# A hybrid decoder layer in float32 pairs: the pooling map goes into the output weight, kept weight parts load from the sync queue

## The chip, the cores and the metric

The kernel runs on one core of a Trainium2 chip. The metric is the device time of one execution in microseconds (us). Five engines work beside each other: TensorE (PE in the profile, its weight loads PEld), VectorE (DVE), ScalarE (ACT), GpSimd (POOL) and SyncE (SP), which here only issues DMAs. A DMA is issued by one of these engines and sits in that engine's queue. Engines meet through semaphores: each runs its own program in order, and what stands behind a wait in it waits too.

## The reference

One decoder layer over 2048 positions of 1024 features, in float32:

```python
z = rmsnorm(h, g_attn) @ w_in              # q (512), k (128), v (128), u (512)
a = sliding_window_sink_attention(norm(q), norm(k), v, sinks, rel_bias)   # window 128, 8 heads of 64
for g, w in enumerate((2, 4, 8, 16)):      # 4 groups of 128 channels
    pooled[g] = mean of the last w positions of u[g] - u[g]
m = einsum('bsgc,gcd->bsgd', pooled, w_pool) * pool_scale
h = h + concatenate([a, m]) @ w_out
h = h + (silu(hn @ w_gate) * (hn @ w_up)) @ w_down           # hn = rmsnorm(h, g_ffn), width 2816
h = h + sigmoid(rmsnorm(h, g_ple) @ w_ple_gate) * (p @ w_ple_proj)
```

## The kernel before

Every float32 operand of a matmul is kept as two parts, hi and lo (`_hi` is a rounded copy, made by ScalarE; `_lo` is the rest, made by VectorE: operand minus hi), and a product is three matmuls: hi x hi, hi x lo, lo x hi. The 2048 positions are four tiles of T = 512.

**Order.** TensorE goes through z(0), z(1), out(0), z(2), out(1), z(3), out(2), out(3), and then twice (for two tiles each) through feed-forward, down projection and gate sections. `z_section(t)` multiplies tile t by w_in: 10 panels of 128x1024 weights, 20 halves, a half being 12 matmuls of 512 columns or 24 of 256. `out_section(t)` multiplies attention and pooling by w_out: 8 panels, 16 halves. Each engine has its own `z_section` and `out_section` with tables that say at which half it does what. Attention of the tile before is spread over the halves in steps (`attention_step`, `hosted`), and TensorE, ScalarE and VectorE each do their part of a step at the same half of their own program. Where a step falls together with the keys and queries of the next block, the transposes of the probabilities are put off into the next half (`put_off`).

**Weight parts.** The panels of z(1) and out(0), indices 10 to 27, are split once; `store_parts` keeps both parts in DRAM (`w_split`). The sections after them load 512 KB of hi and 512 KB of lo for each panel (`load_parts`, on POOL's queue) into three slots (`w_parts`). `load_parts(i)` waits for `panel_used(i - 2)`, so until TensorE has used the panel that held the slot. `OUT_AT` and `Z_AT` are the first panels of a section.

**SP's queue** carries all else: panels that are still to be split, x (`load_chunk`: 256 KB of tile t + 2 in the first two out sections, read by ScalarE and VectorE at halves 2 to 9, `CHUNK_AT = {2 + k: k for k in range(8)}`), stores of h (`store_h1`, 2 MB) and of the normed tiles (`store_n2`, four of 512 KB), in the last out section the feed-forward's inputs (`load_a`, 1 MB each) and first weights (`load_pair`).

**Pooling.** The running sums are POOL's, the mean VectorE's. `pool_y` then multiplies the pooled group by w_pool on TensorE (three matmuls a group and tile, into bank 0, 1, 6 or 7), ScalarE scales the bank into `mix_hi` (L1148) and VectorE makes `mix_lo` (L1772, signal `y_lo`). `out_section` waits for `y_lo`: for the map of group 3 before its second bank, and before each panel of pooling rows. In out(2) the map of tile 3 goes through bank 6, which attention uses too.

**Keys.** Each block of 128 keys is transposed into bank 5; ScalarE copies it to `kT_hi` (L1087), VectorE makes `kT_lo` from bank and `kT_hi` (L1654, signal `kstaged`). The transposes of probabilities (L2405) use bank 5 next, and wait for `kstaged`. `qT_lo` (L1660) comes behind it on VectorE, and the logits (L2392) wait for it. `attend` (L2427, L2428) multiplies the probabilities by the values and waits for `probsT_lo` (L1677).

**VectorE in a z half** does, in this order: the panel's split, `normalise2` (L1572, four pairs at halves 13 to 16; pairs 2 and 3 wait until pairs 0 and 1 have been stored, as they share their buffers), `copy_u` (L1596, which waits for TensorE's panel of that u group), the map's rest, and then the attention step. In an out half it is: `norm_lo` of the chunk (L1560), `add_out` at halves 6, 7, 14 and 15 (L1785, adds two banks to h and so frees them), the attention step. The banks freed at 6 and 7 are written by TensorE at halves 8 and 9. Keys and queries of the next tile's first block are staged at half 9 and wanted at half 11 of out(1).

**Gate sections** take their norm from squares that POOL adds (`acc`, L824). TensorE turns the sum (L2351) behind the first gate panel of the tile before and the resulting scale (L2357) behind the second.

## Time and profile before

| | |
|---|---|
| median of 3 runs | 2053.68 us (2050.17 to 2062.04) |
| the profiled execution | 2053.4 us, its span 2051.5 us |
| TensorE busy | 2011.2 us, 98% of the span |
| VectorE, ScalarE, POOL busy | 67%, 44%, 20% |
| DMA moved | 292.09 MB, mean 142 GB/s |
| granted clock of TensorE | mean 0.998 of full speed |
| w_parts loads on POOL's queue | 88 of 512 KB, 4.8 us to landing (median) |

The profile comes from one execution. TensorE's busy time counts from the start of a matmul to its modelled end; matmuls overlap, so the distance between two starts is shorter than the duration shown. "Idle before" is time in which the engine stood, and the name behind the arrow is what ended it; "issue" means that the profile shows no releaser. PEclk is the granted clock, 1.00 being 2.4 GHz and 0.50 being 1.2 GHz.

### The profile page before, as it was taken

Reading aid. Unit: us, or ns where it says so; the run is one execution under the profiler, and the core shown is the slowest. Engines: PE = TensorE matmul, PEld = TensorE weight load, DVE = VectorE, ACT = ScalarE, POOL = GpSimd, SP = SyncE. Lnnn points to the kernel's source line nnn. Section 1 sums busy time; section 2 is a strip of 40 time slices with the busy share of each in tenths; the row PEclk is TensorE's granted clock in tenths of the full one; section 3 lists DMA queues with packets and bytes.
Section 4 is the critical chain, followed back from the end, with each engine's and each line's share of the span. In section 5 each row is a group of like instructions: output and inputs, shape, how many; then the busy total and the mean of one; then the engine's idle time right before and its main releaser. Section 6 shows DMA issues by size and latency. Waiting matters only on the chain.

```text
span 2051.5 us, 26122 instructions
## 1 busy us (share of the span) xinstructions
PE 2011.2 (98%) x9546; PEld 1663.4 (81%) x9546; DVE 1372.9 (67%) x1920; ACT 899.7 (44%) x1460; POOL 406.5 (20%) x508
## 2 busy tenths in 40 slices
PE   8999999999999999999999999999999999999998
PEld 6887878877788888888888878788888888888877
DVE  4696674767696665655888765966566566987663
ACT  4575754657433333333333543533333333334542
POOL 4454644645410000000000220000000000001310
PEclk9999999999999999999999999999999999999999
DMA  7757566364934223225825128432322328352143
GB/s 193 201 180 245 188 236 219 130 236 131 347 127 130 81 72 103 72 72 171 307 62 165 36 72 223 143 119 67 96 85 72 100 79 292 130 159 78 42 134 103
DMA packets 197387, 292.09 MB, mean 142 GB/s; under 512 B 16139, under 2 KB 118452, under 8 KB 195980
## 3 DMA queue, kind: packets, MB, share of 16 engines
q1 hardware_dynamic: 172672, 212.97, 34.1%
q0 software_dynamic: 22176, 76.96, 10.8%
q8 instruction: 76, 1.25, 0.3%
q10 hardware_dynamic: 2412, 0.50, 0.1%
q14 instruction: 51, 0.42, 0.1%
HBM read 223.25 MB, written 67.51 MB: 142 GB/s over the span
## 4 chain that ended last, share of the span: by engine, by line
PE 84%; DVE 6%; DMA 3%; issue 3%; ACT 2%; POOL 1%; SPq 0%; ACTq 0%; DVEq 0%; POOLq 0%
PE bank L2623 13%; PE bank L2627 13%; PE bank L2625 13%; PE bank L2660 7%; PE bank L2661 7%; PE bank L2662 7%; PE bank L2323 4%; PE bank L2325 4%; PE bank L2324 4%; PE bank L2299 2%; PE bank L2301 2%; PE bank L2300 2%; DMA w_parts<-w_split 1%; PE bank L2392 1%; DVE w_lo L1554 1%
## 5 line engine op out<-in xcount | busy, mean ns | idle before, releaser
L2623 PE MATMUL bank<-a_hi,ring_hi 128*128 128x512 f32 x1232 | 479.7, 389 | 1.0 <-DVE ring_lo L1917 0.7
L2627 PE MATMUL bank<-a_hi,ring_lo 128*128 128x512 f32 x1232 | 479.3, 389 | 0.0
L2625 PE MATMUL bank<-a_lo,ring_hi 128*128 128x512 f32 x1232 | 479.3, 389 | 0.0
L2623 PEld LDWEIGHTS bank<-a_hi,ring_hi 128*128 128x128 f32 x1232 | 231.3, 188 | 49.9 <-DVE ring_lo L1917 1.4
L2625 PEld LDWEIGHTS bank<-a_lo,ring_hi 128*128 128x128 f32 x1232 | 231.3, 188 | 48.0
L2627 PEld LDWEIGHTS bank<-a_hi,ring_lo 128*128 128x128 f32 x1232 | 231.3, 188 | 47.8
L2660 PE MATMUL bank<-d_hi 128*128 128x512 f32 x616 | 239.8, 389 | 0.0
L2662 PE MATMUL bank<-d_hi,d_lo 128*128 128x512 f32 x616 | 239.7, 389 | 0.0
L2661 PE MATMUL bank<-d_lo,d_hi 128*128 128x512 f32 x616 | 239.6, 389 | 0.0
L1376 ACT ACTIVATE d_hi<-keep 128x1024 fp32r<-128x1024 f32 x132 | 139.8, 1061 | 201.9 <-PE bank L2662 184.9
L975 POOL DMA_DIRECT2D hidden_T<-hid x88 | 47.6, 541 | 770.4 <-DVE hid L1953 750.7
L2047 DVE TENSOR_TENSOR d_lo<-keep,d_hi 128x1024 fp32r<-128x1024 f32 x132 | 163.9, 1244 | 52.9 <-ACT d_hi L1376 52.8
L1289 ACT ACTIVATE ring_hi<-raws 128x1024 fp32r<-128x1024 f32 x80 | 84.7, 1058 | 218.5 <-PE bank L2627 208.0
L1917 DVE TENSOR_TENSOR ring_lo<-raws,ring_hi 128x1024 fp32r<-128x1024 f32 x80 | 98.7, 1234 | 99.1 <-ACT ring_hi L1289 99.1
L1554 DVE TENSOR_TENSOR w_lo<-raw,w_hi 128x1024 fp32r<-128x1024 f32 x68 | 87.5, 1287 | 100.4 <-ACT w_hi L1042 100.0
L2662 PEld LDWEIGHTS bank<-d_hi,d_lo 128*128 128x128 f32 x616 | 115.6, 188 | 24.2
L2660 PEld LDWEIGHTS bank<-d_hi 128*128 128x128 f32 x616 | 115.6, 188 | 23.9
L2661 PEld LDWEIGHTS bank<-d_lo,d_hi 128*128 128x128 f32 x616 | 115.6, 188 | 23.8
L824 POOL TENSOR_TENSOR acc<-acc,sq 128x512 f32<-128x512 f32 x72 | 110.8, 1539 | 117.8 <-ACT sq L1049 112.8
L1917 DVE TENSOR_TENSOR ring_lo<-t,ring_hi 128x1024 fp32r<-128x1024 f32 x63 | 77.2, 1226 | 66.7 <-ACT ring_hi L1289 66.7
L1042 ACT ACTIVATE w_hi<-raw 128x1024 fp32r<-128x1024 f32 x68 | 71.8, 1055 | 111.5 <-PE bank L2325 63.3
L1289 ACT ACTIVATE ring_hi<-t 128x1024 fp32r<-128x1024 f32 x63 | 66.5, 1056 | 108.2 <-DVE t L1903 108.2
(258 smaller groups left out, 3879.9 us busy)
## 6 DMA issues: line engine op xcount, KB each, us to landing
w_parts<-w_split POOLq DMA_DIRECT2D x88, 512.0 KB, 4.8
hidden_T<-hid POOLq DMA_DIRECT2D x88, 256.0 KB, 2.3
raws<-in_w_gate SPq DMA_DIRECT2D x80, 256.0 KB, 4.7
raws<-in_w_up SPq DMA_DIRECT2D x80, 256.0 KB, 5.1
keep<-hidden_T SPq DMA_DIRECT2D x66, 256.0 KB, 3.8
raw<-in_w_ple_gate SPq DMA_DIRECT2D x64, 256.0 KB, 4.2
keep<-in_w_down SPq DMA_DIRECT2D x44, 256.0 KB, 4.4
other<-hidden_T SPq DMA_DIRECT2D x44, 256.0 KB, 6.8
```

The lines of the kernel that those rows point to most:

```text
L824: nc.gpsimd.tensor_tensor(into[:, :], slots[:, 0, :] if j == 1 else into[:, :], slots[:, j % 2, :], ALU.add).then_inc(acc_done, 1)
L1289: nc.scalar.activation(ring_of(half, m)[0][:, :, :], ring_source(half, m), ACT.Copy).then_inc(ring_hi_done, 1)
L1376: nc.scalar.activation(d_hi[s % SLOTS][:, :, :], down_pair(s)[0], ACT.Copy).then_inc(d_hi_done, 1)
L1554: nc.vector.tensor_tensor(panel_lo(i), panel_raw(i), panel_hi(i).bitcast(F32), ALU.subtract).then_inc(lo_done, 1)
L1917: nc.vector.tensor_tensor(lo[:, :, :], ring_source(half, m), hi[:, :, :].bitcast(F32), ALU.subtract).then_inc(ring_lo_done, 1)
L2047: nc.vector.tensor_tensor(d_lo[s % SLOTS][:, :, :], down_pair(s)[0], d_hi[s % SLOTS][:, :, :].bitcast(F32), ALU.subtract).then_inc(d_lo_do ...
L2623: mm(dst[:, :], wh[:, g, cols], a_hi[o][:, k, :], start=fresh and k == 0, stop=False, skip_group_check=True)
L2625: mm(dst[:, :], wh[:, g, cols], a_lo[o][:, k, :], start=False, stop=False, skip_group_check=True)
L2627: ins = mm(dst[:, :], wl[:, g, cols], a_hi[o][:, k, :], start=False, stop=k == 3, skip_group_check=True)
L2660: mm(dst, wh[:, cols], ah, start=fresh and k == 0, stop=False, skip_group_check=True)
L2661: mm(dst, wh[:, cols], al, start=False, stop=False, skip_group_check=True)
L2662: ins = mm(dst, wl[:, cols], ah, start=False, stop=k == FPAIRS - 1, skip_group_check=True)
```

## The change

Four things are done.

1. The pooling map is multiplied into the output weight once: rows 512 to 1023 of w_out, scaled by `pool_scale`, are multiplied from the left by w_pool in z(0) (`mix_rows`, 24 matmuls), the product is stored (`w_mixed`, 2 MB) and `out_panel` loads its pooling rows from there. `pool_y`, its copies and its waits are gone; `out_section` waits for the pooled groups themselves (`pool_lo`).
2. `load_parts` moves from POOL's queue to SP's, between SP's other loads and stores; chunks 0 to 3 of tile 3 are issued at the end of z(2) and not in out(1), and the four `load_a` and the loads of h are spread over more panels, with `A_ORDER` to match.
3. ScalarE copies the keys' bank raw to `k_raw` as well as to `kT_hi`; VectorE makes `kT_lo` from `k_raw`, and the transposes wait for `k_hi_done`. In z sections `copy_u` stands behind the attention step, except in halves that begin new logits and in half 19.
4. In gate sections the turn of the squares' sum and all that follows come one panel later.

```diff
-POOL_Z, POOL_Z_COPY = {14: (0,), 16: (1,), 17: (2,), 18: (3,)}, {15: (0,), 17: (1,), 18: (2,), 19: (3,)}
-POOL_O2, POOL_O2_COPY = {9: (0,), 13: (1,), 15: (2,)}, {9: (0,), 13: (1,), 15: (2,)}
-POOL_O3, POOL_O3_COPY = {0: (3,)}, {0: (3,)}
+POOLED_HI_AT, POOLED_LO_AT = {10: 0, 11: 1, 12: 2, 13: 3}, {11: 0, 12: 1, 13: 2, 14: 3}
+POOLED_AT, POOLED_COPY_AT = {13: 0, 14: 1, 15: 2, 16: 3}, {14: 0, 15: 1, 16: 2, 17: 3}
+POOLED_STORE_AT = {16: (0, 1), 17: (2,), 18: (3,)}
...
-A_ORDER = (0, 1, 3, 4, 2, 5, 6)
+A_ORDER = (0, 3, 4, 1, 2, 5, 6)
...
-                return rows(w_out, 2 * r, 2 * r + 2, cols)
+                return rows(w_mixed[:, :], 2 * r - 4, 2 * r - 2, cols)
...
                 sp.wait_ge(n2_done, 4 * t + b + 1)
                 sp.dma_start(hnT_d[t, :, 2 * b:2 * b + 2, :], normed(t, b)).then_inc(n2_stored[b % 2], 16)
+
+            def load_parts(i):
+                kept = (10 + i - OUT_AT[1] if OUT_AT[1] <= i < Z_AT[3] else i - Z_AT[2] if i < Z_AT[3] else
+                        i - Z_AT[3] if i < OUT_AT[2] else 10 + (i - OUT_AT[2]) % 8)
+                if i == SPLIT_END:
+                    sp.wait_ge(lo_done, SPLIT_END)
+                elif i < SPLIT_END + SLOTS_W:
+                    sp.wait_ge(panel_used, SPLIT_END)
+                    for parity in range(2):
+                        sp.wait_ge(parts_stored[parity], 16 * (SPLIT_END - KEPT_FROM))
+                else:
+                    sp.wait_ge(panel_used, i - SLOTS_W + 1)
+                sp.wait_ge(parts_stored[kept % 2], 32 * (kept // 2 + 1))
+                for part in range(2):
+                    sp.dma_start(w_parts[parts_slot(i)][:, part, :].bitcast(F32), w_split[kept, part]
+                                   ).then_inc(parts_landed[parts_slot(i)], 16)
...
                     load_z(t + 1, c)
+                    if t == 1 and c == 0:
+                        load_parts(Z_AT[2] + 1)
+                    if t:
+                        load_parts(Z_AT[t + 1] + c + 2)
...
                     if t == 0 and c in (7, 8):
                         load_chunk(2, 2 * c - 14)
                         load_chunk(2, 2 * c - 13)
+                    if t == 1 and c == 9:
+                        for k in range(4):
+                            load_chunk(3, k)
                     if t == 2 and c >= 9:
                         load_h(2, 0)
                 for c in range(8):
                     load_out(t, c)
-                    if t == 1 and c == 0:
-                        for k in range(4):
-                            load_chunk(3, k)
-                        for b in range(NB):
-                            load_h(1, b)
+                    if t == 0 and c == 7:
+                        load_parts(Z_AT[2])
+                    if t:
+                        load_parts(OUT_AT[t] + c + 2)
+                    if t == 1 and c < 2:
+                        load_h(1, 2 * c)
+                        load_h(1, 2 * c + 1)
                     if t < 2:
                         for k in {3: (4,), 4: (5, 6), 5: (7,)}.get(c, ()):
                             load_chunk(t + 2, k)
...
+                if OUT_AT[3] + c + 2 < ROW_PANELS:
+                    load_parts(OUT_AT[3] + c + 2)
                 if c == 0:
                     store_h1(2)
-                if c == 1:
-                    load_a(0, 0)
-                    load_a(0, 1)
-                    load_a(0, 3)
-                if c == 2:
-                    load_a(0, 2)
+                if 1 <= c < 5:
+                    load_a(0, (0, 2, 1, 3)[c - 1])
                 if c == 4:
...
+                if n:
+                    act.wait_ge(kstaged, n)
+                nc.scalar.activation(k_raw[:, :], bank[5][:, 0:P], ACT.Copy)
                 nc.scalar.activation(kT_hi[:, (b + 1) * P:(b + 2) * P], bank[5][:, 0:P],
                                      ACT.Copy).then_inc(k_hi_done, 1)
...
+            def pooled_rows_hi(g):
+                if g == 0:
+                    act.wait_ge(consts, CONSTS + 16 * NPOOL)
+                nc.scalar.activation(wo_hi[g][:, :], wo_raw[g][:, :], ACT.Copy,
+                                     scale=scale_sb[:, g:g + 1]).then_inc(wp_hi_done, 1)
+
+            def copy_mixed(g):
+                for e in range(2):
+                    act.wait_ge(mixed_bank, 2 * g + e + 1)
+                    nc.scalar.activation(mixed[g][:, e * T:(e + 1) * T], mixed_bank_of(g, e)[:, :],
+                                         ACT.Copy).then_inc(mixed_copied, 1)
...
-                nc.vector.tensor_tensor(kT_lo[:, cols], bank[5][:, 0:P], kT_hi[:, cols].bitcast(F32),
+                nc.vector.tensor_tensor(kT_lo[:, cols], k_raw[:, :], kT_hi[:, cols].bitcast(F32),
                                         ALU.subtract).then_inc(kstaged, 1)
...
                         normalise2(t - 2, SCALE2_AT[half])
-                    for g in U_COPY_AT[t > 0].get(half, ()):
+                    fresh = any(has_unit(k, 0) and k % 2 == 0 for _, k in hosted_steps("z", t, half))
+                    u_first = fresh or half == 19 or not late
+                    for g in U_COPY_AT[t > 0].get(half, ()) if u_first else ():
                         copy_u(t, g)
...
-                        for g in POOL_Z_COPY.get(half, ()):
-                            pool_y_rest(t - 1, g)
+                    if t == 0 and half in POOLED_LO_AT:
+                        pooled_rows_lo(POOLED_LO_AT[half])
+                    if t == 1 and half == 5:
+                        dve.wait_ge(mixed_stored, 16 * NPOOL)
                     hosted("z", t, half, Z_AT[t] + half // 2 + 1 if half % 2 == 0 and late else None)
+                    for g in () if u_first else U_COPY_AT[t > 0].get(half, ()):
+                        copy_u(t, g)
 
...
-                            if r == 1:
+                            if r == 2:
                                 sum_squares(NORM3[g + 1], bank[BS0[0]])
-                            if r == 2:
+                            if r == 3:
                                 normalise3(g + 1, 0)
                                 normalise3(g + 1, 1)
                                 norm3_lo(g + 1, 0)
-                            if r == 3:
                                 norm3_lo(g + 1, 1)
...
-                pe.wait_ge(kstaged, 4 * s + min((k + 1) // PAIRS + 1, NB))
+                pe.wait_ge(k_hi_done, 4 * s + min((k + 1) // PAIRS + 1, NB))
...
-                if n >= 48 and n % 16 in (7, 11, 13):
-                    pe.wait_ge(y_lo, {7: 13, 11: 14, 13: 15}[n % 16])
...
+            def mix_rows(g):
+                pe.wait_ge(wp_lo_done, g + 2)
+                if g == 0:
+                    pe.wait_ge(kvcopied, NB)
+                elif g >= 2:
+                    pe.wait_ge(mixed_copied, 2 * g - 2)
+                for e in range(2):
+                    dst, cols = mixed_bank_of(g, e), slice(e * T, (e + 1) * T)
+                    mm(dst[:, :], wp_hi[:, g, :], wo_hi[g][:, cols], start=True, stop=False)
+                    mm(dst[:, :], wp_hi[:, g, :], wo_lo[g][:, cols], start=False, stop=False)
+                    mm(dst[:, :], wp_lo[:, g, :], wo_hi[g][:, cols], start=False, stop=True
+                       ).then_inc(mixed_bank, 1)
 
...
+                        mix_rows(POOLED_AT[half])
                     hosted("z", t, half)
...
                         elif first and t < 3:
                             pe.wait_ge(ucopied, 4 * t + 4 + b + 1)
-                            if b < 2:
-                                pe.wait_ge(y_lo, 4 * t + 3 + b)
...
                     if e == 0 and r >= 2 and part == 0:
-                        pe.wait_ge(y_lo, 4 * t + 2 * r - 2)
+                        pe.wait_ge(pool_lo, 4 * t + 2 * r - 2)
...
                             if not second and e == 0 and part == 1:
-                                if r == 0:
+                                if r == 1:
                                     pe.wait_ge(pp_copied, 8 * g + 4 + 1)
                                     turn_squares(NORM3[g + 1], acc3, bank[BS0[0]])
-                                if r == 1:
+                                if r == 2:
                                     pe.wait_ge(pp_copied, 8 * g + 4 + 2)
                                     turn_rstd(NORM3[g + 1], bank[BS0[1]])
```

## Rows read from the trace of the kernel before

**Rows 1.** The page: busy time of the engines; what the DMA moved in 40 slices.

```profile
PE 2011.2 (98%) x9546; PEld 1663.4 (81%) x9546; DVE 1372.9 (67%) x1920; ACT 899.7 (44%) x1460; POOL 406.5 (20%) x508
...
GB/s 193 201 180 245 188 236 219 130 236 131 347 127 130 81 72 103 72 72 171 307 62 165 36 72 223 143 119 67 96 85 72 100 79 292 130 159 78 42 134 103
```

**Rows 2.** Waits of TensorE: waited for, us in total, times, longest.

```profile
PE bank L2405 <- issue: 4.5, 4, 1.9
...
PE bank L2427 <- issue: 4.2, 3, 1.6
...
PE bank L2323 <- DVE mix_lo L1772: 3.1, 2, 1.8
...
PE bank L2351 <- POOL acc L824: 2.6, 2, 1.3
...
PE bank L2299 <- DMA w_parts<-w_split: 2.1, 1, 2.1
...
PE bank L2323 <- DMA w_parts<-w_split: 1.9, 2, 1.5
...
PE bank L2323 <- DVE wide_lo L1772: 1.0, 1, 1.0
...
PE bank L2427 <- DVE wide_lo L1772: 0.7, 1, 0.7
```

**Rows 3.** Timeline of second output section: start us, us, engine, line [idle before <-releaser].

```profile
315.48 1.10 POOL L858 DMA_DIRECT2D w_parts<-w_split  x2 [0.38 <-PE bank L2325]
...
316.54 0.72 ACT L1056 ACTIVATE wide_hi<-stage,gains 128x512 fp32r<-128x512 f32 x1 [0.54 <-DMA stage<-in_x]
...
316.58 0.69 DVE L1785 TENSOR_TENSOR h<-bank,h 128x512 f32<-128x512 f32 x1 [0.92 <-PE bank L2325]
...
320.92 1.10 POOL L858 DMA_DIRECT2D w_parts<-w_split  x2 [1.58 <-PE bank L2325]
```

**Rows 4.** Timeline of TensorE, one pooling group in z section 2.

```profile
275.43 0.48 PE L2484 MATMUL bank<-mix_hi,wp_hi 128*128 128x512 f32 x1
...
276.22 0.40 PE L2340 MATMUL bank<-wide_hi,w_parts 128*128 128x512 f32 x1
```

**Rows 5.** Timeline of z section 3, VectorE and TensorE.

```profile
369.78 0.29 DVE L1654 TENSOR_TENSOR kT_lo<-bank,kT_hi 128x128 fp32r<-128x128 f32 x1
...
370.17 0.63 PE L2405 MATMUL bank<-ident,scores 128*128 128x128 f32 x4 [1.93 <-issue]
...
370.79 0.68 DVE L1660 TENSOR_TENSOR qT_lo<-bank,qT_hi 128x512 fp32r<-128x512 f32 x1
```

**Rows 6.** Windows behind that: us, busy us by engine, PEclk, DMA share, GB/s.

```profile
371.00:375.00 4.00, 4.00 (x22) 2.93 (x21) 1.70 (x6) 2.33 (x7) 3.37 (x6) 0.57 0.67 229
```

**Rows 7.** Two lines of VectorE: duration ns min/median/max, first and last start.

```profile
L1654 DVE TENSOR_TENSOR kT_lo<-bank,kT_hi x16: 279/291/293, 78.6 to 488.6; 128x128 fp32r<-128x128 f32 x16
...
L1717 DVE TENSOR_TENSOR mix_lo<-share,mix_hi x24: 411/426/1532, 100.0 to 429.6; 128x256 fp32r<-128x256 f32 x24
```

**Rows 8.** Timeline of z section 1, half 17 of VectorE, half 18 of TensorE.

```profile
149.91 0.69 DVE L1596 TENSOR_TENSOR u<-bank,spread 128x512 f32<-128x512 f32 x1
...
151.25 0.74 DVE L1772 SCALAR_TENSOR_TENSOR mix_lo<-bank,scale_sb,mix_hi 128x512 fp32r<-128x512 f32 x1
...
153.56 0.36 PE L2427 MATMUL bank<-probsT_hi,vv 128*128 128x256 f32 x1 [1.64 <-issue]
```

**Rows 9.** DMA issues in 70.5:73 and in 313:316: xcount, KB each, us to landing.

```profile
raw<-in_w_in SPq DMA_DIRECT2D x2, 256.0 KB, 4.8
...
stage<-in_x SPq DMA_DIRECT2D x2, 256.0 KB, 2.9
```

**Rows 10.** Timeline of z section 2, halves 15 and 16.

```profile
281.88 1.12 POOL L858 DMA_DIRECT2D w_parts<-w_split  x2 [0.28 <-issue]
...
285.64 1.41 DVE L1572 SCALAR_TENSOR_TENSOR stage<-h,gains,spread 128x512 f32<-128x512 f32 x2
```

**Rows 11.** Timeline of the first gate section, second gate panel.

```profile
1205.17 2.22 DVE L1554 TENSOR_TENSOR w_lo<-raw,w_hi 128x1024 fp32r<-128x1024 f32 x1 [4.29 <-ACT w_hi L1042]
...
1207.53 0.73 PE L2323 MATMUL bank<-hn_hi_first,w_hi 128*128 128x512 f32 x1 [0.45 <-DVE w_lo L1554]
```

More of the change, by code:

```diff
@@ L938, in z_section @@
                         powers(NORM1[1])
+                    if t == 0:
+                        for g in POOLED_STORE_AT.get(half, ()):
+                            store_mixed(g)
+                    if t == 1 and half == 4:
+                        pool.wait_ge(mixed_stored, 16 * NPOOL)
                     if t >= 2:
@@ L1198, in z_section @@
                         nc.scalar.activation(wp_hi[:, :, :], wp_raw[:, :, :], ACT.Copy).then_inc(wp_hi_done, 1)
+                        for g in range(NPOOL):
+                            act.dma_start(wo_raw[g][:, :], w_out[QW + g * P:QW + (g + 1) * P, :]).then_inc(consts, 16)
                     if t == 0 and 8 <= half < 16:
```

111 lines of the change are left out of this document (37 added, 74 removed).

## The prediction

> **What bounds the kernel now.** I read the page first: TensorE is busy for 2011.2 of 2051.5 us and no other engine for more than 67% [rows 1]. So the time is TensorE's own work and the 40 us in which it stands. Next the list of what TensorE waited for [rows 2]; every part of the change can be held against one of its lines. Its busy time is modelled, so I count work by the distance between starts in the timeline. In the second `out` section (`out` 1) POOL's load for half 6 left at 315.48, 0.38 us after TensorE freed its slot, and that for half 8 at 320.92, some 0.4 us after [rows 3]: a half panel of 12 matmuls takes 2.7 us, 0.23 each. Last I followed each wait in the timeline, to see which instruction of which queue ended it and what would be late next. The profiled execution took 2053.4 us, 1.9 more than its span, and 0.3 less than the median of the runs; the sum is made against 2053.4.
>
> **The map, multiplied into the weight.** Before, each of 16 pooling groups costs TensorE three matmuls: from 275.43 to 276.22, 0.79 us [rows 4], 16 x 0.78 = 12.5 us in all. After, `mix_rows` does 4 rows x 2 halves = 8 such groups once, 8 x 0.74 = 5.9 us. That is **-6.6 us** of work. The copies that go with it (16 on ScalarE, 16 on VectorE, about 0.7 us each) lie beside TensorE. The new ones (4 weight splits, 8 bank copies) fall in the first z section, where ScalarE's queue also loads 2 MB of w_out rows beside SP's panels, and POOL's stores 2 MB; ScalarE, VectorE and POOL wait for those stores in z section 1, some 20 us after they left. Panels land there some 2 to 4 us before they are split, so I charge 0.5 us, from 0 to 3.
>
> With the map go its waits: `out` no longer waits for `y_lo`, lines L2323 <- L1772 with 3.1 and 1.0 us and L2427 <- L1772 with 0.7 [rows 2], **-4.8 us**. `pool_lo`, which takes their place, is signalled halves earlier. Two of the 16 groups save nothing, though: in the second half of z sections 2 and 3 `attend` waits for VectorE (part of the 4.2 us of "issue" at L2427), and VectorE is busy without a break there; TensorE arrives 0.8 us earlier and waits 0.8 longer: **+1.6 us**.
>
> **The keys' raw copy.** In z section 3 VectorE ends kT_lo at 370.07 and the put-off transposes start at 370.17, after 1.93 us of idle time called "issue" [rows 5]: they waited for `kstaged`. The four such waits sum to 4.5 us [rows 2]. Now they wait for ScalarE's `k_hi_done`, which comes earlier. But what is late next? The next logits need qT_lo, which VectorE ends at 371.47 [rows 5] and which nothing makes earlier. TensorE, free at 368.2, would be there after 0.35 us of transposes and 6 matmuls, at 370.0. So 1.5 of the 1.9 us come back later. Only in z section 1, where `copy_u` now stands behind the attention step, is the whole wait (1.0) won. With 0.4 here and 0.3 at its like in `out` 2 I take **-1.7 us** of the 4.5 (bounds 0 and -4.5). After this gap TensorE ran with a mean granted clock of 0.57, that is at 1.2 GHz for 3.4 us [rows 6], which costs 1.7 us; whether a gap of 1.6 us still brings it is open: -0.8.
>
> The subtraction kT_lo took 0.28 to 0.29 us in all 16 places while it read a bank; the like one on two SBUF tiles, mix_lo at L1717, takes 0.43 and up to 1.53 us [rows 7]. The Trainium skill (SBUF — State Buffer, section "SBUF: two separate sides") says that a VectorE operation with two SBUF inputs and a GpSimd one lock each other out. It speaks against this edit, and the trace agrees with it; by it the 16 subtractions would take up to 1 us more each, all of it VectorE's.
>
> **`copy_u` behind the attention step.** In z section 1 `attend` waited 1.64 us, with the map's rest (0.74 us, at 151.25) and `copy_u` (0.69 us) ahead of the attention step on VectorE [rows 8]. Both are gone from there: **-1.4 us**.
>
> **Weight parts on the sync queue.** POOL is rid of 88 issues; that alone lies on no path. TensorE waited 2.1 and 1.9 us for w_parts [rows 2]. The first lies at the head of z section 2, where two panels and the 2 MB store of h left together; the other late one is in the last `out`, behind that store and 3 MB of `load_a`. SP in order now sends the store, and the `load_a`s one at a time, behind the parts. I take **-3.4 us** of 4.0.
>
> The price is that SP waits. `load_parts(i)` waits for `panel_used(i - 2)`, and all behind it in SP's program waits too. In `out` 1, chunk 4 is now sent behind parts that wait until the third panel is used (half 6 begins, 315.1), chunks 5 and 6 until the fourth (half 8, 320.5), chunk 7 until the fifth. But `norm_hi` needs them at halves 6, 7, 8 and 9; before, only the squares of earlier chunks held them back. VectorE does norm_lo(4) before `add_out` 0 and 1, and norm_lo(5) before `add_out` 2 and 3, and these free the banks that TensorE wants at halves 8 and 9. How long from the release to the landing? Two issues of 512 KB take POOL 1.1 us [rows 3], and where SP sent a panel behind such a pair in z section 1, its two loads landed 4.8 us (median) after their own issue, the first a little before [rows 9]: 1.0 + 4.5 = 5.5 us. Then ScalarE 0.7, VectorE 0.7, `add_out` 0.7 [rows 3]:
> - chunk 4 lands at 320.6, bank 0 is free at 322.6, wanted at 320.5: 2.1 us.
> - chunk 5 lands at 326.0, bank 2 is free at 328.1, wanted at 322.6 + 2.7 = 325.3: 2.8 us.
> - chunk 7 is released at 330.9, lands at 336.4; behind it on ScalarE and VectorE stands the first `stage_k` and `stage_q` of tile 2 (now with the extra copy), ready at 339.7, wanted at 336.9: 2.8 us.
>
> **+7.7 us.** Bounds: 0 if a chunk lands 2.9 us after its release, as chunks 6 and 7 did after their issue when nothing stood ahead on SP's queue [rows 9]; 11 if each comes a microsecond later. I stay near the middle, as the 1 MB ahead is certain. Three gaps of 2 to 3 us can bring the low clock as the one above did: +0.7. The skill (DMA: Bandwidth & Descriptors, section "SWDGE vs HWDGE vs iDMA") says that the engines take turns between the hardware and software queues; by it a chunk on SP's queue shared the engines with POOL's parts before, and now stands behind them. No row here shows the turns themselves.
>
> In z sections 2 and 3 the store of normed pair 1 no longer leaves as soon as it is normed but when the eighth panel is used (281.6, where POOL's load left at 281.88), and lands 5.4 us later, at 287.0. `normalise2(_, 3)`, which waits for its buffer, started at 285.64 [rows 10]. The `attend` that follows on VectorE's work had no slack, so TensorE gets it 1.2 us later, and the 0.8 us of the map's group before it are lost again: 2 x 2.0 = **+4.0 us** (0 to 5).
>
> In the last `out` the first gate and up blocks are sent only after the last parts and the stores of tile 2 have landed. From half 8 on, 5 MB pass on SP's queue before them (parts, one `load_a`, two stores, parts, two stores). At 3.0 us for 1 MB (347 GB/s in slice 11 [rows 1]) that is 15 us and 1.7 to land; the first block 3.2 later; then ScalarE 1.1, VectorE 1.2 and one `add_out` 0.7: 22.9, and the first product of the feed-forward wants it after 8 halves, 21.8. **+1.5 us** with what follows (0 to 5).
>
> **The gate's norm, a panel later.** TensorE waited 1.3 us twice for acc. But w_lo of the next panel ended only at 1207.39 and TensorE waited for it 0.45 us more [rows 11]. Without the turn it waits there for w_lo all the same, and the four transposes (0.45 us) are no longer hidden: **+0.9 us** for both. VectorE's split of panel 7 becomes late by up to 0.4 us, inside the bounds. Bounds: -2.6 and +2.
>
> **A_ORDER** follows the order in which the blocks now land; nothing.
>
> **Sum:** -6.6 - 4.8 + 1.6 - 1.7 - 0.8 - 1.4 - 3.4 + 0.5 + 7.7 + 0.7 + 4.0 + 1.5 + 0.9 = -1.8. 2053.4 - 1.8 = 2051.6; I say 2051.5 us.
>
> **Rivals.**
> 1. *The chunks land in time*: SP's queue alone is quick enough, or ScalarE's wait is elsewhere. For it: 2.9 us were seen [rows 9]; against it, 1 MB stands ahead. Then the 8.4 us of `out` 1 and half of the 4.0 us fall away: 2041.2. Faster. Chance 0.27.
> 2. *SP's queue moves 1 MB in 5 us, not 3*, as one pair of parts took on POOL's (4.8 on the median in the page): then the 5 MB of the last `out` cost 10 us more, and the 1 MB ahead of each of three chunks 2 us more each: 2051.5 + 16 = 2067.5, slower. It decides from about 4.6 us on, as each further us for 1 MB costs 8. Against it: 347 GB/s over a whole slice. Chance 0.13.
> 3. *The keys' and norms' waits go wholly* (-2.8, -3.5): if VectorE, rid of 12 us of work, runs ahead. 2045.3. A part of my own case's range; it alone would not pass the bound of 0.5%.
>
> **Chances.** A measurement of this kernel tells about 0.5%, 10.3 us, from no change: faster is below 2043.4, slower above 2063.9. The likeliest case, 18.7 us of gains of which SP's order gives back 13.9, holds 0.60, by itself 2044.5 to 2058. Faster 0.27, same 0.60, slower 0.13. The range goes from just under rival 1 to the upper bounds of the three SP terms: 2040 to 2062.
>
> **What would show it.** TensorE's waits for L1772 and the 12.5 us at L2484 are gone, and 24 matmuls stand in z section 0. In `out` 1 there are new waits at halves 8 and 9 ended by `add_out` and at half 11 ended by qT_lo, 2 to 3 us each; their absence makes me wrong. The transposes' wait moves to L2392. The wait for acc turns into one for w_lo. If the store of h no longer meets the parts, the head of z section 2 has no DMA wait.

## The result, and the profile after

The changed kernel takes 2060.05 us (median of 20 runs, 2054.24 to 2067.09), the kernel before 2053.59 us in runs on the same chip. The ratio is 1.0031, 95% interval 1.0021 to 1.0041: slower by 6.4 us, inside the range of the prediction and within 0.5%, but with the other sign than its 2051.5 us. The profiled execution took 2059.9 us, its span is 2058.1 us, against 2053.4 and 2051.5. Medians here are over all executions and ratios over the fast ones alone; one execution of stores_first (2227.53 us) and one of turn_back (4094.16 us) were slow.

The page of the kernel after answers [rows 1]:

```profile
PE 2007.4 (98%) x9522; PEld 1661.7 (81%) x9522; DVE 1371.1 (67%) x1908; ACT 901.1 (44%) x1472; POOL 363.5 (18%) x424
...
GB/s 222 227 183 239 226 214 184 164 207 188 315 131 120 100 67 92 87 72 165 310 62 165 25 68 232 147 118 67 97 83 72 104 77 296 122 162 73 41 133 103
```

TensorE's busy time fell by 3.8 us, and yet the span grew by 6.6. The list of its waits answers [rows 2]; its columns are the same.

```profile
PE bank L2425 <- DVE qT_lo L1692: 9.8, 6, 4.2
PE bank L2356 <- DVE w_lo L1586: 5.1, 3, 2.4
PE bank L2356 <- DVE h L1816: 4.2, 1, 4.2
PE bank L2458 <- issue: 4.1, 4, 1.7
PE bank L2642 <- DVE h_last L1816: 2.4, 1, 2.4
PE bank L2458 <- DVE probsT_lo L1709: 2.1, 3, 0.9
PE bank L2384 <- POOL acc L856: 1.8, 1, 1.8
```

All three lines for L1772 (the map's rest) and both for w_parts are gone, and so is "issue" at the transposes. In their place stand qT_lo (9.8 us), `add_out` (L1816: 4.2 and, on `h_last`, 2.4), probsT_lo and w_lo in the gate sections (L2356, 5.1). To see the places I took the distance between the first matmuls of the sections, which holds work, waits and slow clock alike, and beside it the sum of the prediction's terms for that stretch:

| stretch | before | after | difference | predicted |
|---|---|---|---|---|
| up to the end of z(0) | 70.8 | 77.6 | +6.8 | +6.4 |
| z(1), out(0) | 139.9 | 134.1 | -5.8 | -7.3 |
| z(2) | 85.7 | 83.3 | -2.4 | -2.3 |
| out(1) | 50.0 | 60.2 | **+10.2** | +7.1 |
| z(3) | 88.8 | 83.6 | -5.2 | -1.5 |
| out(2), out(3), up to the end of TensorE's last matmul there | 122.8 | 117.3 | -5.6 | -6.5 |
| first 200 matmuls of the feed-forward, with the wait ahead of them | 45.0 | 52.2 | **+7.2** | +1.5 |
| the rest, both gate sections in it | | | +1.3 | +0.9 |

Two stretches lose 17.4 us. Each figure is from one profile. Three other kernels of the experiments run the same program up to the end of z(0), and there the growth was 5.6 to 7.4 us; two of them, stores_first and turn_back, are the same in out(1) as well, and it grew by 11.1 and 8.9 us there.

The timeline of out(1) answers [rows 3] (SPq is SP's queue issuing):

```profile
312.38 0.38 SPq L579 DMA_DIRECT2D stage<-in_x  x1
...
318.83 0.72 ACT L1073 ACTIVATE wide_hi<-stage,gains 128x512 fp32r<-128x512 f32 x1 [14.55 <-DMA stage<-in_x]
...
320.25 1.28 DVE L1816 TENSOR_TENSOR h<-bank,h 128x512 f32<-128x512 f32 x2
...
321.08 0.77 PE L2356 MATMUL bank<-mix_hi,w_parts 128*128 128x512 f32 x1 [4.18 <-DVE h L1816]
...
330.00 0.38 SPq L579 DMA_DIRECT2D stage<-in_x  x1
...
338.57 0.69 DVE L1692 TENSOR_TENSOR qT_lo<-bank,qT_hi 128x512 fp32r<-128x512 f32 x1 [0.20 <-ACT qT_hi L1116]
...
339.32 0.43 PE L2425 MATMUL bank<-kT_hi,qT_hi 64*128 64x256 f32 x2 [4.21 <-DVE qT_lo L1692]
```

Chunk 4 left at 312.38, behind the parts, and landed when ScalarE took it, 6.4 us later. norm_lo and the first `add_out` followed, and TensorE, which wanted bank 0 at 316.9, stood for 4.18 us. Four halves later it was the same with chunk 7, sent at 330.00, which held back the queries of the next tile.

The DMA issues in 311.4 to 318.5 answer [rows 9]: behind a pair of parts a chunk took 4.9 us, not the 2.9 that it took on an empty queue.

```profile
stage<-in_x SPq DMA_DIRECT2D x3, 256.0 KB, 4.9
```

The windows (columns as in [rows 6]) behind these two waits, in the new kernel's z section 3, and behind a wait in the first gate section:

```profile
321.00:326.00 5.00, 4.92 (x12) 3.94 (x13) 3.14 (x5) 2.38 (x4) 2.40 (x3) 0.51 0.34 127
...
339.00:344.00 5.00, 4.68 (x22) 3.84 (x23) 2.79 (x12) 2.03 (x8) 1.46 (x2) 0.66 0.08 30
380.00:384.00 4.00, 3.68 (x30) 3.33 (x31) 2.10 (x9) 3.40 (x10) 3.34 (x6) 1.00 0.88 257
1213.00:1217.00 4.00, 4.00 (x12) 3.10 (x12) 2.36 (x2) 1.20 (x2) 0.00 (x0) 0.57 0.53 133
```

After 4.18 us of waiting the granted clock was 0.51 for 5 us (1.2 GHz for almost all of it), after 4.21 us it was 0.66. Where it was low a matmul started every 0.43 us instead of every 0.23, so these two windows cost about 2.4 and 1.7 us. In z section 3, where it was 0.57 before, it is 1.00.

The timeline at the head of the feed-forward:

```profile
551.62 0.39 SPq L654 DMA_DIRECT2D raws<-in_w_gate  x1
...
555.51 1.06 ACT L1321 ACTIVATE ring_hi<-raws 128x1024 fp32r<-128x1024 f32 x1 [8.45 <-DMA raws<-in_w_up]
...
556.60 1.23 DVE L1953 TENSOR_TENSOR ring_lo<-raws,ring_hi 128x1024 fp32r<-128x1024 f32 x1 [6.30 <-ACT ring_hi L1321]
...
558.57 0.47 PE L2642 MATMUL bank<-a_hi,ring_hi 128*128 128x512 f32 x1 [2.45 <-DVE h_last L1816]
...
562.02 1.06 ACT L1321 ACTIVATE ring_hi<-raws 128x1024 fp32r<-128x1024 f32 x1 [1.82 <-DMA raws<-in_w_up]
...
564.79 1.14 ACT L1066 ACTIVATE sq<-h_last 128x512 f32<-128x512 f32 x2
...
565.49 6.36 POOL L856 TENSOR_TENSOR acc<-acc,sq 128x512 f32<-128x512 f32 x4 [3.00 <-ACT sq L1066]
...
571.91 0.66 PE L2384 MATMUL bank<-ident,acc 128*128 128x128 f32 x4 [1.76 <-POOL acc L856]
```

The first gate block left at 551.62, where the kernel before sent it at 544.16; its split stands ahead of `add_out` on VectorE, and TensorE waits 2.45 us. Behind it the second block's split on ScalarE waits for its DMA, and the rest of the last tile's squares stand behind that split (and behind one of an input block, 1.90 us, as before), POOL's sums behind the squares, and the turn of the sum at the end of the line, 1.76 us late.

The timeline of the remaining places, in order of time: the last three matmuls of the map's first row block and the half behind them (for [rows 4]), the attention of z section 1 ([rows 8]), the stores of normed pairs ([rows 10]), the keys of z section 3 ([rows 5]), the second gate panel ([rows 11]).

```profile
55.85 0.39 PE L2508 MATMUL bank<-wo_hi,wp_hi 128*128 128x512 f32 x1
...
56.53 0.39 PE L2373 MATMUL bank<-wide_hi,w_hi 128*128 128x512 f32 x1
...
157.15 0.36 PE L2458 MATMUL bank<-probsT_hi,vv 128*128 128x256 f32 x1 [0.57 <-issue]
...
279.20 2.37 SPq L548 DMA_DIRECT2D ffn_in_T<-stage  x2
...
285.70 1.40 DVE L1604 SCALAR_TENSOR_TENSOR stage<-h,gains,spread 128x512 f32<-128x512 f32 x2
...
376.86 0.60 PE L2438 MATMUL bank<-ident,scores 128*128 128x128 f32 x4
...
378.46 0.28 DVE L1686 TENSOR_TENSOR kT_lo<-k_raw,kT_hi 128x128 fp32r<-128x128 f32 x1
...
379.58 0.69 DVE L1692 TENSOR_TENSOR qT_lo<-bank,qT_hi 128x512 fp32r<-128x512 f32 x1
...
380.32 0.38 PE L2425 MATMUL bank<-kT_hi,qT_hi 64*128 64x256 f32 x2 [1.48 <-DVE qT_lo L1692]
...
1210.40 2.22 DVE L1586 TENSOR_TENSOR w_lo<-raw,w_hi 128x1024 fp32r<-128x1024 f32 x1 [4.30 <-ACT w_hi L1059]
...
1212.76 0.47 PE L2356 MATMUL bank<-hn_hi_first,w_hi 128*128 128x512 f32 x1 [2.40 <-DVE w_lo L1586]
```

Three matmuls of the map take 0.68 us, eight such groups a little under 6. The attention's wait fell from 1.64 to 0.57 us. `normalise2` of the last pair starts at 285.70, where it started at 285.64. The transposes at 376.86 no longer wait, kT_lo starts 1.6 us after them, and the wait of 1.93 stands now at the logits as 1.48 us for qT_lo. The wait for acc is gone, and w_lo alone costs 2.40 us, where it was 1.31 for acc and 0.45 for w_lo.

### The profile page after: what moved, and what is told of

The parts are those of the page before. It is cut to its first block, busy times and chain, and to the rows that moved or that the text cites. A ratio compares the mean times of both kernels' runs of the same rounds, so it can differ in the third digit from the quotient of the medians.

```text
span 2058.1 us, 26077 instructions
## 1 busy us (share of the span) xinstructions
PE 2007.4 (98%) x9522; PEld 1661.7 (81%) x9522; DVE 1371.1 (67%) x1908; ACT 901.1 (44%) x1472; POOL 363.5 (18%) x424
## 3 DMA queue, kind: packets, MB, share of 16 engines
q8 instruction: 76, 1.25, 0.3%
## 4 chain that ended last, share of the span: by engine, by line
PE 83%; DVE 6%; ACT 4%; DMA 3%; issue 3%; POOL 1%; SPq 0%; ACTq 0%; DVEq 0%; POOLq 0%
PE bank L2642 13%; PE bank L2644 13%; PE bank L2646 13%; PE bank L2679 7%; PE bank L2681 7%; PE bank L2680 7%; PE bank L2356 5%; PE bank L2358 5%; PE bank L2357 5%; PE bank L2332 1%; PE bank L2334 1%; PE bank L2333 1%; PE bank L2425 1%; DMA raw<-in_w_in 1%; DVE stage L1604 1%
## 5 line engine op out<-in xcount | busy, mean ns | idle before, releaser
L2644 PEld LDWEIGHTS bank<-a_lo,ring_hi 128*128 128x128 f32 x1232 | 231.3, 188 | 47.8
```

What stands on the lines that cost most here:

```text
L2644: mm(dst[:, :], wh[:, g, cols], a_lo[o][:, k, :], start=False, stop=False, skip_group_check=True)
```

## The experiments

Each line: median, and ratio to the kernel before on the same chip with its 95% interval. The kernel before took 2053.59 us beside after, 2053.29 beside the next four, 2053.00 beside parts_alone, map_alone, keys_alone and sp_mended, and 2054.11 beside h_later and the three whose names begin with mended; across these groups the ratios are to be compared. All are written out below.

| kernel | us | ratio |
|---|---|---|
| after | 2060.05 | 1.0031 (1.0021 to 1.0041) |
| chunks_first | 2048.03 | 0.9971 (0.9959 to 0.9983) |
| stores_first | 2056.15 | 1.0013 (1.0004 to 1.0022) |
| turn_back | 2055.29 | 1.0007 (0.9997 to 1.0016) |
| parts_on_pool | 2053.09 | 1.0002 (0.9993 to 1.0011) |
| parts_alone | 2069.42 | 1.0079 (1.0065 to 1.0093) |
| map_alone | 2048.57 | 0.9980 (0.9971 to 0.9989) |
| keys_alone | 2050.57 | 0.9990 (0.9980 to 1.0000) |
| sp_mended | 2040.76 | 0.9936 (0.9922 to 0.9950) |
| mended_no_map | 2048.78 | 0.9974 (0.9963 to 0.9985) |
| h_later | 2049.66 | 0.9979 (0.9971 to 0.9988) |
| mended_a_late | 2042.63 | 0.9945 (0.9933 to 0.9957) |
| mended_turn_later | 2043.58 | 0.9943 (0.9931 to 0.9955) |

**chunks_first.** The chunks of out(1) leave ahead of the parts:

```diff
+                    if t == 1:
+                        for k in {2: (4, 5), 4: (6, 7)}.get(c, ()):
+                            load_chunk(3, k)
                     if t:
                         load_parts(OUT_AT[t] + c + 2)
...
-                    if t < 2:
+                    if t < 1:
                         for k in {3: (4,), 4: (5, 6), 5: (7,)}.get(c, ()):
```

> The kernel after, with chunks 4 and 5 of tile 3 sent ahead of the parts that SP sends at c = 2 and chunks 6 and 7 ahead of those at c = 4, instead of behind the parts of c = 3 to 5. Theory A (the chunks stand behind parts whose release they must wait for): the stretches of out 1 that grew against the kernel before (half 7 by 4.3 us, half 8 by 2.3, half 11 by 4.8, half 12 by 1.0, sum 12.4) go back; about 2048 us. Rival B (SP's queue carries too much there in any order, so the wait moves to w_parts): waits of 1 to 3 us for DMA at two or three panels of out 1; 2055 to 2060 us.

SP's issues in its timeline:

```profile
303.74 0.80 SPq L579 DMA_DIRECT2D stage<-in_x  x2
...
306.30 6.24 SPq L563 DMA_DIRECT2D w_parts<-w_split  x4
...
312.62 3.17 SPq L579 DMA_DIRECT2D stage<-in_x  x2
```

out(1) fell from 60.2 to 48.3 us, and the time by 12.0. Theory A holds; in this order the parts cost 0.3 us of waiting in the whole kernel.

**stores_first.** The stores of tile 2's normed rows leave at c = 4, ahead of the parts:

```diff
+                if c == 4:
+                    store_n2(2, 0)
+                    store_n2(2, 1)
+                    store_n2(2, 2)
+                    store_n2(2, 3)
                 if OUT_AT[3] + c + 2 < ROW_PANELS:
                     load_parts(OUT_AT[3] + c + 2)
...
-                if c == 4:
-                    store_n2(2, 0)
-                    store_n2(2, 1)
                 if c == 5:
-                    store_n2(2, 2)
-                    store_n2(2, 3)
                     load_pair(0, 0, (0, 1))
```

> The kernel after, with the four stores of tile 2's normed rows sent ahead of the parts of panel 6 of the last out section (half 8) instead of behind them and load_a, so that the first gate and up blocks can leave earlier. Theory A (the first blocks left 7.5 us later than before because the stores they wait for stood behind 3 MB of other transfers): the blocks leave at about 545 instead of 551.6, the 7 us lost between the end of out 3 and the 200th matmul of the feed-forward fall to 1 or less; about 2053.5 us. Rival B (the blocks must wait for the same bytes in any order): no more than 2 us are won, 2058 to 2060 us.

The first block left at 543.31, 8.3 us earlier, and the wait for `h_last` is gone. But 3.9 us were won (the medians), not 7: the stretch from the first to the 200th matmul fell only from 49.3 to 47.9 us, against 44.8 before. The first blocks landed 8 to 9.5 us after their issue, since the last load of a (1 MB) and two pairs of parts had left only just ahead of them. Between both theories; what remained is taken up by mended_a_late.

**turn_back.** The turn of the gate's norm is in its old panels (`r == 0`, 1, 2 for turn, scale and normalising, instead of 1, 2, 3).

> The kernel after, with the turn of the gate's norm (TensorE's transposes and what follows on ScalarE and VectorE) in the panels where it was before. Theory A (the wait for acc only turned into one for w_lo, 2.4 us, long enough to bring 3.4 us of half clock at the second place, where the kernel before had none): the waits for acc of 1.3 us and for w_lo of 0.45 us return, 2.0 us gained at the second place, 0.7 at the first, 1.5 lost a hundred us behind the first; about 2058.5 us. Rival B (the turn a panel later was worth the 1.3 us waits it removes): 2061 to 2062.5 us.

4.8 us won, more than the 1.5 of Theory A, and the intervals of the two ratios do not meet. In the profiles 3.6 us lie at the gates (0.7, 0.5 and 2.3, the last with the slow clock at the second gate gone), 1.4 in out(1), which this edit does not touch. mended_turn_later repeats it on another base.

**parts_on_pool.** SP's and POOL's programs as in the kernel before, all else as after.

> The kernel after, with the kept weight parts loaded by POOL's queue as before, and SP's program and A_ORDER as before; map, keys' raw copy, copy_u and the gate's turn stay changed. Theory A (the order on SP's queue costs 12.4 us in out 1, 7 at the start of the feed-forward and 1 to 2 at the normed stores, and brings 3.4 us of waits for w_parts): about 2042.5 us. Rival B (the waits belong to the earlier arrival of TensorE, not to the queue: with the map gone it runs into the same chunks and blocks): 2048 us or more.

A miss of 10.6 us for Theory A; Rival B holds. out(1) took 54.9 us, not 50, z(3) 85.0 and out(3) 1.8 more than after. TensorE's waits in that kernel show why:

```profile
PE bank L2357 <- DMA w_parts<-w_split: 6.5, 2, 4.4
...
PE bank L2333 <- DMA w_parts<-w_split: 2.0, 1, 2.0
```

The w_parts waits, 4.0 us before, are 8.5 now. A slow clock follows two of them. The wait at the head of out(1) is 4.4 us where it had been 0.43: TensorE comes 2.3 us earlier (294.1 against 296.4) and no longer stands for the map's rest, while the parts for its second panel still land at 304, behind 3 MB of chunks and h that SP sent from 289.7 on. So the rest of the change meets a wall in out(1) that the queue move takes away. Whatever the order on SP's queue costs, moving the parts there costs 7.0 us when the rest of the change is in (2060.05 against 2053.09).

**parts_alone** and **map_alone** put that to the test from the other side: the kernel before with the move to SP alone, and with the map and `copy_u` alone.

> The kernel before with one part of the change: the kept weight parts loaded by SP's queue, in the order of the kernel after (its chunk loads, loads of a and A_ORDER too). Theory A (each part of the change has its own price, which add up): 12.4 us lost in out 1, 7 at the start of the feed-forward, 2 at the normed stores, 4 won for w_parts: about 2070 us. Rival B (the parts interact: the kernel before comes to these places later, with its waits for the map's rest, so that part of the lateness is covered): 2060 to 2066 us.

> The kernel before with the pooling map multiplied into the weight and copy_u behind the attention step, nothing else of the change. Theory A (TensorE comes to out 1 some 2 us earlier and there meets the parts on POOL's queue, which land no earlier behind 4 MB of chunks and h: the 4.4 us wait for w_parts and the slow clock after it, seen with the parts back on POOL, take back half of the gain): 2050 to 2052.5 us. Rival B (the terms of the prediction add up as they stand, -6.6 -4.8 +1.6 -1.4 +0.5): 2042.6 us.

The move alone costs 16.4 us (my terms for it sum to +10.5): Theory A for this time, though not for the kernels together, as the same move costs 7.0 us above. The map brings 4.4 (my terms: 10.7); that is 1.4 us below the bracket of Theory A and 6 above Rival B, so what is taken back, 6.3 us, is a little over the half that A has. TensorE's waits in map_alone, where 6.4 us stand for w_parts in out sections instead of 1.9:

```profile
PE bank L2355 <- DMA w_parts<-w_split: 6.4, 2, 4.4
```

In parts_alone the row of `normalise2` shows the stall that I had predicted for the normed stores, 0.61 us there (1.25 in z section 3). In the kernel after it is 0, as shown above:

```profile
288.38 1.42 DVE L1571 SCALAR_TENSOR_TENSOR stage<-h,gains,spread 128x512 f32<-128x512 f32 x2 [0.61 <-DMA ffn_in_T<-stage]
```

**keys_alone.** The raw copy alone.

> The kernel before with the keys' raw copy on ScalarE alone (k_raw, kT_lo from it, the transposes waiting for ScalarE's kT_hi). Theory A (the transposes' waits of 4.5 us move for the most part to the next logits' wait for qT_lo): -1 to -2.5 us, 2051 to 2052.3 us, with L2405's waits gone and new ones for qT_lo of 1.5 us. Rival B (the waits go wholly): 2048.8 us. Rival C (the subtraction with two SBUF inputs is longer by up to 1 us, VectorE later by as much in the second half of z sections 2 and 3): 2054 us or more.

-2.4 us, Theory A, though the interval reaches up to no change. In the profiles half 5 of z section 3 took 7.24 us instead of 9.30; 0.45 us of this is the shorter wait (1.48 instead of 1.93), the other 1.6 the slow clock behind it, which did not come this time. Rival C is not the verdict, but it is at work; see the last section.

**sp_mended.** Both reorderings, the loads of a at c = 1, 2, 2, 3, the stores of normed pairs 1 and 2 ahead of the parts of c = 8, the turn back.

> The kernel after with four things mended on top of each other: the chunks of tile 3 ahead of the parts (as in chunks_first), the stores of tile 2's normed rows ahead of the parts of panel 6 (as in stores_first) with the four loads of a leaving at c = 1, 2, 2 and 3 instead of 1 to 4, the stores of normed pairs 1 and 2 in z sections 2 and 3 ahead of the parts sent at c = 8, and the gate's turn in its old panels. Theory A (the losses have separate places and add up: 12 in out 1, 4 to 6 at the start of the feed-forward, 1.8 for two waits of 0.9 for probsT_lo in z sections 2 and 3, 2.4 for the turn): about 2039 us. Rival B (a stall that goes brings the next one, as with the parts back on POOL's queue): 2044 us or more. The start of the feed-forward alone: with the loads of a earlier the stretch from the second to the 200th matmul comes back to 45 us if the squares of the last tile waited on ScalarE behind a late first split; it stays at 48 if it is something else.

2040.8 us: 19.3 us below the kernel after, 12.2 below the one before. Theory A, but for one term. TensorE's waits:

```profile
PE bank L2432 <- DVE qT_lo L1698: 5.1, 5, 1.7
...
PE bank L2465 <- DVE probsT_lo L1715: 2.0, 3, 0.9
PE bank L2363 <- DMA w_parts<-w_split: 1.1, 1, 1.1
```

The 2.0 us for probsT_lo are still there with the normed stores ahead of the parts. So those stores cost the kernel after nothing, and the waits are the map's own: TensorE arrives earlier at work of VectorE that is no earlier. The mean granted clock is 1.000 (after: 0.995); this profile is of the fastest of six executions (2036.56 us), the others had 0.998 to 1.000.

**mended_no_map**, **mended_a_late** and **mended_turn_later** take one thing away from it (mended_no_map and map_alone take or keep `copy_u`'s new place together with the map); the edit of mended_a_late:

```diff
-                for which in {1: (0,), 2: (2, 1), 3: (3,)}.get(c, ()):
-                    load_a(0, which)
+                if 1 <= c < 5:
+                    load_a(0, (0, 2, 1, 3)[c - 1])
```

> The kernel sp_mended without the map's part: the map is applied per tile as in the kernel before; parts on SP's queue in the mended order and the keys' raw copy stay. Theory A (with the parts landing in time the map is worth its work and its waits, about 10 us): 2050 to 2052 us. Rival B (the map is worth the 4.4 us that it brought alone): 2045 us.

> The kernel sp_mended with the four loads of a at c = 1 to 4, as in the kernel after. Theory A (the a that lands last pushes the first gate and up blocks back, and the squares of the last tile stand behind their splits on ScalarE): the stretch from the second to the 200th matmul of the feed-forward grows from 45.5 to 48 us, the 1.1 us wait for w_parts in the last out section goes; 2042 to 2042.5 us. Rival B (the loads of a do not matter): 2040.8 us.

> The kernel sp_mended with the gate's norm turn one panel later, as in the change. Theory A (at both places a wait of 1.3 us for acc and one of 0.45 us for w_lo turn into one of 2.4 us for w_lo, 0.65 us more, and another 1.6 us at each place where the clock then runs low): 2042 to 2045.5 us. Rival B (the turn later is worth the waits for acc, 2.6 us): 2038 us.

By the ratios the map is worth 7.8 us on this base, between both theories. That is 3.4 more than it brings alone, but the intervals leave this difference within the noise; what speaks for it is the trace of map_alone with its longer waits for w_parts. The late loads of a cost 1.8 us by the ratios, whose intervals overlap, so the time alone decides nothing. The profiles do: the first 200 matmuls of the feed-forward took 45.5 us in all three kernels with the early loads and 47.8 here (47.9 in stores_first, where they are late too), and the wait of 1.1 us for w_parts went. That is Theory A. The turn costs 1.4 us by the ratios (2.8 by the medians), and these intervals overlap as well, so the size is open, but no gain is to be seen. The windows around its two gates, each with a wait of 2.4 us:

```profile
1195.00:1201.00 6.00, 3.67 (x16) 3.07 (x17) 4.54 (x3) 3.77 (x6) 1.10 (x1) 1.00 0.39 91
1941.00:1945.00 4.00, 4.00 (x13) 3.13 (x12) 2.36 (x2) 0.95 (x2) 0.00 (x0) 0.63 0.67 141
```

**h_later.** Is it the 3 MB (my expectation says 4) that hold the parts back when POOL sends them? Against parts_on_pool, beside the gate's turn in its old panels:

```diff
-                        for b in range(NB):
-                            load_h(1, b)
+                    if t == 1 and c in (4, 5):
+                        load_h(1, 2 * c - 8)
+                        load_h(1, 2 * c - 7)
```

> Map, keys' raw copy and copy_u as in the kernel after, parts on POOL's queue, the gate's turn where it was, and the four loads of h for tile 1 sent by SP at c = 4 and 5 of out 1 instead of right behind the chunks at its start. Theory A (the parts of panel 1 of out 1 wait behind 4 MB of chunks and h on the shared engines; with 2 MB ahead they land 3 to 5 us earlier): the 4.4 us wait for w_parts and the 2.5 us of slow clock go, out 1 falls from 54.9 to about 48.5 us, 2044 us in all. Rival B (POOL's queue itself is slow): out 1 stays above 52 us, 2049 to 2051 us.

out(1) took 55.2 us and the whole 2049.66. My Theory A fell, and the times are Rival B's. The first pair of parts did land 3.3 us earlier (300.7 instead of 304.0), and the wait only moved one panel on:

```profile
295.67 1.18 POOL L868 DMA_DIRECT2D w_parts<-w_split  x2
...
301.45 2.33 POOL L879 TENSOR_TENSOR qrs<-qms,minus_half 128x10 f32<-128x10 f32 x1
303.73 2.24 POOL L868 DMA_DIRECT2D w_parts<-w_split  x4
...
310.94 0.77 PE L2359 MATMUL bank<-mix_hi,w_parts 128*128 128x512 f32 x1 [4.40 <-DMA w_parts<-w_split]
```

POOL sends the next parts at 303.73, because the rows of the norms of queries and keys (L874 and L879, the last of them 2.33 us) stand ahead in its program; the panel had been free since 300.9. They land at 310.8. So two things hold the parts back on POOL's queue: SP's bytes, as this run shows, and POOL's own work, as its trace is read; no run takes that work away. With the move to SP no wait for w_parts is left in the trace.

## Why the prediction was wrong

**Right, and shown.** The waits for L1772 and w_parts are gone; the transposes' wait moved to the next logits, as said, with 1.5 of 1.9 us coming back in z section 3; the waits in out(1) are ended by `add_out` and by qT_lo, though they are two of 4.2 us and not three of 2 to 3; the wait for acc turned into one for w_lo. z section 0 grew by 6.8 us (6.4). SP's order is what costs: parts_alone, chunks_first and stores_first show it apart.

**The steps that failed are two sizes.** *The start of the feed-forward*, +1.5 us, measured +7.2. The way to the first product was nearly right: from half 8 (534.1) the last store landed after 17.5 us, where I had 15 and 1.7, the blocks that ScalarE waited for landed 3.9 later and not 3.2, and TensorE waited 2.45 us, where 22.9 against 21.8 gave 1.1. What I had left out is the rest, for which the term has 0.4: the squares of the last tile stand on ScalarE behind the split of the second block, so a late block is paid again at the turn of the sum (1.76), at u (0.5) and at cg (0.8, before 0.3), and the first 200 matmuls took 49.3 us instead of 44.8. *The chunks of out(1)*, 7.7 + 0.7, measured as 12.4 over its four grown halves (4.3, 2.3, 4.8, 1.0). The waits themselves are 4.18 + 4.21 = 8.4, near the 7.7. The other 4 are slow clock, for which I had 0.7: I took its price from one wait of 1.93 us and did not ask what 4 us of standing bring. Together these two sizes are 9.7 us, and more than the 8.3 us between the sum (2051.6) and the profiled execution (2059.9).

**Errors that went the other way.** The stores of normed pairs, +4.0, cost nothing. I let SP's store of pair 1 leave at 281.6, when the eighth panel was used; it left at 279.20, right behind the parts, which TensorE's last matmul with that panel released ahead of the attention step of half 15 and its wait of 1.67 us. The trace of before had it too: there this matmul ended at 279.14, and POOL's load, which I took for the moment, left 2.7 us later. The store landed at 285.5, and `normalise2` started at 285.70. It was a near thing: in z section 3 the store landed at 428.95 and `normalise2` started at 428.97, and in parts_alone it is late by 0.61 and 1.25 us. This +4.0 in the sum is a part of why the total missed by less than the two sizes, and that part is luck. Against that, of the 3.1 us of map work in the second half of z section 2 some 1.8 came back as waits (I had 0.8). The slow clock of z section 3 went wholly (1.6, I had 0.8), which by the last section may be luck.

**The sum was wrong as a sum.** The prices of the parts depend on each other. The queue move costs 16.4 us in the kernel before and 7.0 with the rest of the change in, a difference of 9 to 10 us that is clear of the noise. Put the other way, the rest of the change (map, keys, turn) is worth 9.4 us with the parts on SP's queue (parts_alone against after) and nothing with them on POOL's (parts_on_pool against before). The other parts measure alone -4.4 (map), -2.4 (keys) and, on the mended base, +1.4 to +2.8 (turn); all four add up to +11 to +12.4, where the change measures +6.4. The reason lies in the traces: the parts on POOL's queue come no earlier when TensorE does. I had booked the queue move's gain as the 4.0 us of waits that the trace of before shows; with the map gone those waits would have been 8.5. In the same way the 2.05 us won at the head of z section 2 were given back for the most part four halves later: half 5 grew from 5.87 to 7.25 us with a wait of 1.49 for qT_lo.

**Rivals.** That the chunks land in time was wrong as the change has it, and became true with them ahead of the parts (chunks_first, 2048.0). That 1 MB takes 5 us on SP's queue was wrong: in the last `out` the DMA engines moved from 534.1 on without a break and had passed the 5 MB by 549.7, so 3.1 us for 1 MB; a loss in that place came all the same, by another road. Of the third rival the norms' half came true, for the reason above and not by a faster VectorE; the keys' half did not.

**Open.** Of the turn a panel later the sign is shown (turn_back), the size is not: 4.8 us on the kernel after, 1.4 to 2.8 on the mended one. What brings the slow clock after a short wait is not settled either.

## What to carry to other kernels

A queue is a program in order: before a load that waits for a buffer is put into it, list what stands behind it and when that is wanted. The same bytes in another order were worth 12 us here, and 19.3 with all four mendings, of which the gate's turn moves no bytes. And a wait in a trace is the price of being late at the present arrival times: when one part of a change makes the critical engine earlier, redo the waits of every other part with the new times instead of adding up the old ones.

## What the runs showed of the hardware

**The length of a short wait does not tell the clock behind it.** In the gate sections of the fourteen profiles, waits of 1.3 to 1.6 and of 0.45 us close together were followed by a low granted clock at 10 of 18 places, and single waits of 2.4 to 2.7 us at 7 of 10; each time it cost 1.6 us or so. The two windows of mended_turn_later above show it both ways after the same wait of 2.4 us. A wait of 1.93 us brought it in z section 3 of the kernel before, and the same wait in the same place of parts_alone did not (half 5 took 7.82 us, not 9.30). In the profile of sp_mended, whose longest wait behind the start is 1.7 us, it never came. Waits of 4.0 to 4.4 us are another matter: there are nine in the fourteen profiles, all in out(1), and the clock was at 1.2 GHz behind every one of them, in some from before the end of the wait on (in after from 319.0 to 326.0, the wait having ended at 321.08). So for a short wait a profile in which the slow clock shows is one draw; for one of 4 us its price belongs into the sum.

**VectorE with two SBUF inputs waits for GpSimd.** kT_lo, made from `k_raw` and `kT_hi` instead of from the bank, for [rows 7]:

```profile
L1686 DVE TENSOR_TENSOR kT_lo<-k_raw,kT_hi x16: 277/292/1164, 85.4 to 490.8; 128x128 fp32r<-128x128 f32 x16
```

In the kernel before all sixteen took 0.28 to 0.29 us, though seven of them ran beside a GpSimd tensor operation too. Now seven take 331 to 1164 ns, each of them begun while a GpSimd tensor operation was running, together 2.9 us more. keys_alone, where nothing else is changed, has seven as well, 2.3 us more in all:

```profile
L1658 DVE TENSOR_TENSOR kT_lo<-k_raw,kT_hi x16: 277/293/1167, 78.7 to 486.9; 128x128 fp32r<-128x128 f32 x16
```

The longest, in out(2):

```profile
490.50 1.28 POOL L856 TENSOR_TENSOR acc<-sq 128x512 f32<-128x512 f32 x1 [1.02 <-ACT sq L1066]
...
490.78 1.16 DVE L1686 TENSOR_TENSOR kT_lo<-k_raw,kT_hi 128x128 fp32r<-128x128 f32 x1 [0.42 <-ACT kT_hi L1107]
```

GpSimd's operation ends at 491.78, VectorE's at 491.94. It is so in all seven places: VectorE's ends 0.15 to 0.16 us after the GpSimd operation beside it. Two of the nine short ones began 0.12 us before the end of a GpSimd copy and ended 0.15 us after it, within their usual time. By this the kernel after pays in z section 1 (kT_lo 1.14 us, then a wait for qT_lo of 0.80 where I had counted 1.0 us as wholly won) and in out(2), where the wait grew from 1.46 to 1.68. The Trainium skill (SBUF — State Buffer, section "SBUF: two separate sides") says that the port pair the two engines share is held by whichever of the two starts first for its whole instruction, for a VectorE operation with two SBUF inputs against a GpSimd one that reads SBUF. The trace agrees, with these durations. The prediction named the rule and did not charge it.
